# Requesting the third expert's weights together with the first two, before the routing ends

## The chip, the cores and the metric

The kernel runs on one core of a Trainium2 chip. The metric is the device time of one execution in microseconds, lower is better. The engines are TensorE (PE in the rows, its weight loads PEld), VectorE (DVE), ScalarE (ACT), GpSimd (POOL) and SyncE (SP). SyncE does nothing but wait and issue transfers here. Transfers of all queues run on the core's 16 DMA engines.

## The reference

Two layers over 256 context tokens and 512 latent tokens of width 1024. Each layer has a mixer (retention and a linear recurrence in the first, latent attention in the second) and then a hierarchical mixture of experts, in f32. Only the experts matter here:

```python
def hier_moe(h, group_w, group_b, expert_w, expert_b, w_gate, w_up, w_down):
    """h (T,D). Top-1 expert group, then top-2 experts inside it; exact sorted dispatch."""
    ...
    xin = h[row_tok].reshape(n_blocks, MOE_BLOCK, d)

    def expert_block(args):
        xb, e = args
        return (jax.nn.silu(xb @ w_gate[e]) * (xb @ w_up[e])) @ w_down[e]
```

There are 32 experts with a hidden width of 512, so each has three matrices of 2048 KB: gate, up and down. The first layer routes 768 tokens, the second the 512 latent tokens; each token goes to two experts. A block holds at most 128 rows.

## The kernel before

An expert layer is `moe_rows`. It reserves three buffers for each kind of weights (`expert_weights(s, 3)`: `moew_wg`, `moew_wu`, `moew_wd` in the rows) and calls `routing`, then `experts`.

**Routing.** VectorE works out which expert gets which token, with a few small matmuls in between, and last casts the list of tokens to integers (`all_tok`). SyncE has nothing to do but `prefetch`, which is the function `first` of `moe_rows`: it requests gate, up and down weights of experts 0 and 1, six transfers. At the end of the routing all engines meet.

**Experts.** The 32 experts are taken in order, one turn each, expert n in buffer n modulo 3 (q). Engines meet by semaphores only:

- GpSimd copies the indices of a turn (`exp_idx`) and issues an indirect transfer, the gather, that brings the expert's rows of `h_rows` to one of three buffers `xg` (in the space `all_hT`). It gathers 64 rows if the expert has 64 tokens or fewer, otherwise 128. `x_ready[q]` tells that they have landed. The first three gathers are issued at once, each further one when TensorE has transposed a buffer's rows.
- TensorE transposes the rows (`exp_xps`, line 1793), multiplies them with the gate and up weights (`exp_gps` and `exp_ups`, lines 1806 and 1807), transposes the rows of the next expert, then transposes the hidden rows (`exp_hps`) and multiplies them with the down weights (`exp_yps`, lines 1822 and 1824). Experts with 64 rows or fewer put the two products side by side on the array and take about half the time.
- ScalarE and VectorE form the hidden rows and copy results out of PSUM; ScalarE issues the store to `ys`.
- SyncE requests weights, through `load_gate_up` (line 1684, two transfers) and `load_down` (line 1690). Once TensorE is done with expert n's gate and up weights (`gu_used`), it requests those of expert n + 3 into the same buffer, and after `d_used` the down weights.

The weights of expert 2, the third, are requested at the head of SyncE's part of `experts`, behind a wait for the first gather:

```python
            sp.wait_ge(x_ready[0], 16)
            load_gate_up(sp, a, layer, w, S - 1, S - 1)
            load_down(sp, a, layer, w, S - 1, S - 1)
```

After the experts come `further_blocks` (for rows beyond 128 of an expert; the profile has no transfer of it) and `combine`, which gathers each token's two rows of `ys`.

Of the kernel before, what the change touches and what calls it, by code (L numbers as in the profile page):

```python
# [1668 lines left out]
def expert_weights(s, slots):  # L1669

    w = Box()
    w.g = [s.sb(f"wg{i}", [P, KD, HID]) for i in range(slots)]
    w.u = [s.sb(f"wu{i}", [P, KD, HID]) for i in range(slots)]
    w.d = [s.sb(f"wd{i}", [P, HT_N, DM]) for i in range(slots)]
    w.gu_ready = [s.sem(f"gu_ready{i}") for i in range(slots)]
    w.d_ready = [s.sem(f"d_ready{i}") for i in range(slots)]
    return w


def load_gate_up(sp, a, layer, w, e, q):  # L1680

    for buf, name in ((w.g, "moe_w_gate"), (w.u, "moe_w_up")):
        src = a[name][layer].rearrange("e (p k) n -> e p (k n)", p=P)[bass.ds(e, 1)]
        sp.dma_start(buf[q][:].rearrange("p k n -> p (k n)"), src.rearrange("o p m -> (o p) m")).then_inc(w.gu_ready[q], 16)


def load_down(sp, a, layer, w, e, q):

    src = a["moe_w_down"][layer].rearrange("e (p k) n -> e p (k n)", p=P)[bass.ds(e, 1)]
    sp.dma_start(w.d[q][:].rearrange("p k n -> p (k n)"), src.rearrange("o p m -> (o p) m")).then_inc(w.d_ready[q], 16)  # L1690


def experts(nc, c, a, layer, t0, r, w):
# [3 lines left out]
    with Scope(nc, f"exp{layer}") as s:  # L1697
        S = len(w.g)
# [18 lines left out]
        x_ready = [s.sem(f"x_ready{i}") for i in range(S)]  # L1717
# [24 lines left out]
        @block.sync  # L1742
        def _(sp):


            sp.wait_ge(x_ready[0], 16)
            load_gate_up(sp, a, layer, w, S - 1, S - 1)
            load_down(sp, a, layer, w, S - 1, S - 1)

            def turn(n, q, i):  # L1750
                sp.wait_ge(gu_used, n + 1)
                load_gate_up(sp, a, layer, w, n + S, q)
                sp.wait_ge(d_used, n + 1)
                load_down(sp, a, layer, w, n + S, q)

            with sp.Fori(0, E // S - 1) as i:
                for q in range(S):
                    turn(i * S + q, q, i)
            for n in range((E // S - 1) * S, E - S):
                turn(n, n % S, n // S)  # L1760
# [403 lines left out]
def moe_rows(nc, c, a, layer, t0, r):  # L2164

    with Scope(nc, f"moew{layer}") as s:
        w = expert_weights(s, 3)

        def first(sp):

            for e in range(len(w.g) - 1):
                load_gate_up(sp, a, layer, w, e, e)
                load_down(sp, a, layer, w, e, e)

        routing(nc, c, a, layer, t0, r, first)
        experts(nc, c, a, layer, t0, r, w)
    further_blocks(nc, c, a, layer, t0, r)
# [116 lines left out]
```

## Time and profile before

| | |
|---|---|
| median of 3 runs | 2321.19 us |
| lowest and highest | 2316.5 and 2325.09 us |
| profiled execution | 2321.44 us |
| its span, first to last instruction | 2319.8 us |
| mean granted TensorE clock | 0.919 of full speed |
| TensorE matmuls busy | 1889.0 us, 81% |
| VectorE busy | 716.2 us, 31% |
| weights requested by SyncE, 64 experts | three transfers of 2048 KB each |
| mean over the span | 246 GB/s of HBM traffic |

The profile is that of the profiled execution, and all times in rows are microseconds from its first instruction. The two expert layers take about half of the span. A queue's time from issue to landing includes the time that the transfer stood behind others.

### The profile page before, as it was taken

The numbers are of one execution on the slowest core, as the hardware profiler recorded it, in microseconds if no ns is written. First come the engines' busy times: TensorE is split into PE (matmuls) and PEld (weight loads), VectorE is DVE, ScalarE is ACT, GpSimd is POOL, SyncE is SP. The second block draws the span as 40 slices with busy tenths as digits, with TensorE's granted clock in tenths as the row PEclk, the third lists the DMA queues.
The fourth block names the chain that finished last, engine by engine and source line by source line (L and its number), as shares of the span: only waits on it lengthen the run. The fifth ranks groups of instructions, "written<-read, shape, count | busy, mean of one in ns | idle before, by whom it ended". The sixth has DMA issues, their size and how long they took to land. (4 is left out here: it accounts for less than half of the span.)

```text
span 2319.8 us, 23218 instructions
## 1 busy us (share of the span) xinstructions
PE 1889.0 (81%) x7918; PEld 982.4 (42%) x7919; DVE 716.2 (31%) x1243; ACT 429.8 (19%) x748; POOL 279.3 (12%) x355
## 2 busy tenths in 40 slices
PE   2559999889489999999853899999957989987781
PEld 0125444555334444444412546888533334433330
DVE  1130678553411111111227226555331111111114
ACT  2000233311001111111113114444201111111112
POOL 1020254211110000000014010000011000000001
PEclk9779999989689999999985899999968999998896
DMA  9971119210588999999963102000159999999993
GB/s 369 422 261 43 36 60 248 100 58 28 235 339 342 398 409 412 420 386 371 400 260 142 55 0 82 1 1 1 49 219 357 408 411 402 394 402 395 401 414 132
DMA packets 93246, 572.21 MB, mean 247 GB/s; under 512 B 21016, under 2 KB 35096, under 8 KB 61304
## 3 DMA queue, kind: packets, MB, share of 16 engines
q1 hardware_dynamic: 76864, 515.04, 56.7%
q0 software_dynamic: 8832, 30.68, 3.9%
q10 hardware_dynamic: 7480, 25.57, 2.8%
q8 instruction: 43, 0.70, 0.1%
q14 instruction: 27, 0.22, 0.0%
HBM read 529.47 MB, written 41.78 MB: 246 GB/s over the span
## 5 line engine op out<-in xcount | busy, mean ns | idle before, releaser
L1806 PE MATMUL exp_gps<-moew_wg,all_hT 128*64 128x512 f32 (+1 forms) x1024 | 486.1, 615 | 36.8 <-DMA moew_wu<-in_moe_w_up 34.7
L1807 PE MATMUL exp_ups<-moew_wu,all_hT 128*64 128x512 f32 (+1 forms) x1024 | 484.4, 613 | 0.0
L1806 PEld LDWEIGHTS exp_gps<-moew_wg,all_hT 128*64 128x64 f32 (+1 forms) x1024 | 153.4, 153 | 325.9 <-issue 321.0
L1822 PE MATMUL exp_yps<-moew_wd,all_hT 128*64 128x512 f32 (+1 forms) x512 | 243.7, 607 | 39.5 <-issue 39.5
L1824 PE MATMUL exp_yps<-moew_wd,all_hT 128*64 128x512 f32 (+1 forms) x512 | 244.2, 608 | 0.0
L1916 DVE TENSOR_TENSOR all_hT<-all_hT,exp_ups 64x512 f32<-64x512 f32 (+1 forms) x64 | 44.2, 691 | 586.4 <-ACT all_hT L1867 586.4
L1807 PEld LDWEIGHTS exp_ups<-moew_wu,all_hT 128*64 128x64 f32 (+1 forms) x1024 | 154.2, 153 | 50.9 <-issue 50.9
L577 PE MATMUL abp_ps<-abp_w,all_hT 128*128 128x512 f32 x384 | 166.8, 593 | 0.9 <-PE abp_ps L577 0.6
L1925 DVE COPY exp_y<-exp_yps 64x512 f32<-64x512 f32 (+1 forms) x64 | 44.3, 692 | 298.4 <-PE exp_yps L1824 298.4
L1822 PEld LDWEIGHTS exp_yps<-moew_wd,all_hT 128*64 128x64 f32 (+1 forms) x512 | 71.5, 149 | 147.9 <-issue 147.9
L1867 ACT ACTIVATE all_hT<-exp_gps 64x512 f32<-64x512 f32 (+1 forms) x64 | 37.8, 591 | 485.4 <-PE exp_ups L1807 485.4
L215 PE MATMUL ada_ps<-ada_w,ada_sT 128*32 128x512 f32 x384 | 63.2, 818 | 74.8 <-DMA ada_w<-in_ada_w 74.8
L577 PEld LDWEIGHTS abp_ps<-abp_w,all_hT 128*128 128x128 f32 x384 | 72.7, 190 | 93.7 <-issue 93.5
L1772 POOL COPY exp_idx<-all_tok 128x1 int32 (+1 forms) x64 | 11.7, 183 | 799.5 <-DVEq L1906 798.7
L1872 ACT COPY exp_y<-exp_yps 64x512 f32<-64x512 f32 (+1 forms) x64 | 37.2, 581 | 381.4 <-PE exp_yps L1824 381.4
L1321 PE MATMUL att_sc<-mla_KT,mlak_QT 96*128 96x384 f32 x256 | 98.0, 507 | 2.0 <-PEq L75 2.0
L581 PE MATMUL abp_ps<-all_hT,abp_w 128*128 128x256 f32 (+1 forms) x256 | 85.6, 498 | 15.8 <-DMA abp_w<-in_ab_w_in 15.5
L1793 PE MATMUL exp_xps<-all_ident,all_hT 128*128 128x128 f32 x512 | 74.5, 290 | 25.6 <-DMA all_hT<-h_rows,exp_idx 25.6
L1793 PEld LDWEIGHTS exp_xps<-all_ident,all_hT 128*128 128x128 f32 x512 | 64.3, 194 | 71.9 <-issue 46.0
L1332 PE MATMUL att_pv<-mla_V,mla_ckT 128*128 128x64 f32 x768 | 92.7, 271 | 0.0
L1332 PEld LDWEIGHTS att_pv<-mla_V,mla_ckT 128*128 128x128 f32 x768 | 90.7, 192 | 0.0
L1824 PEld LDWEIGHTS exp_yps<-moew_wd,all_hT 128*64 128x64 f32 (+1 forms) x512 | 72.5, 149 | 24.9 <-issue 24.9
(368 smaller groups left out, 2264.3 us busy)
## 6 DMA issues: line engine op xcount, KB each, us to landing
moew_wg<-in_moe_w_gate SPq DMA_DIRECT2D x64, 2048.0 KB, 23.1
moew_wu<-in_moe_w_up SPq DMA_DIRECT2D x64, 2048.0 KB, 29.0
moew_wd<-in_moe_w_down SPq DMA_DIRECT2D x64, 2048.0 KB, 27.7
ada_w<-in_ada_w SPq DMA_DIRECT2D x12, 4096.0 KB, 25.6
ys<-exp_y ACTq DMA_DIRECT2D x51, 256.0 KB, 8.3
abp_w<-in_ab_w_in SPq DMA_DIRECT2D x6, 2048.0 KB, 8.2
ys<-abp_zero SPq DMA_DIRECT2D x32, 256.0 KB
ys<-exp_y ACTq DMA_DIRECT2D x13, 512.0 KB, 10.1
```

The lines of the kernel that those rows point to most:

```text
L215: last = nc.tensor.matmul(ps[n % 2][32 * j:32 * j + 32, :], sT[:, k_, :], w[m % WB][:, kk, j * 512:(j + 1) * 512], start=(k_ == 0), stop=( ...
L577: last = nc.tensor.matmul(ps[i % RB][:], hT[:, kk, what * P:(what + 1) * P], w[n % S][:, kk, :], start=(kk == 0), stop=(kk == KD - 1))
L581: last = nc.tensor.matmul(ps[i % RB][:, 0:m], w[n % S][:, kk, ct * P:(ct + 1) * P], hT[:, kk, o:o + m], start=(kk == 0), stop=(kk == KD - 1))
L1321: last = nc.tensor.matmul(sc[n % 2][:, b, 0:HALF], k.QT[0:QD, h, t * P:(t + 1) * P], k.KT[0:QD, h, b * HALF:(b + 1) * HALF], start=True, s ...
L1332: last = nc.tensor.matmul(pv[n % 2][:, 0:VD], pT[n % 2][:, kt, :], k.V[:, kt, h * VD:(h + 1) * VD], start=(kt == 0), stop=(kt == NT - 1))
L1793: last = nc.tensor.transpose(xps[k // 4][:, k % 4, :], x_by[q][:, k, :], c.ident[:])
L1806: nc.tensor.matmul(gps[0:rows, :], x[:, k, 0:rows], w.g[q][:, k, :], start=(k == 0), stop=(k == KD - 1))
L1807: last = nc.tensor.matmul(ups[at:at + rows, :], x[:, k, 0:rows], w.u[q][:, k, :], start=(k == 0), stop=(k == KD - 1))
L1822: nc.tensor.matmul(yps[0][0:rows, :], hT[:, k, 0:rows], w.d[q][:, k, 0:512], start=(k == 0), stop=(k == HT_N - 1))
L1824: last = nc.tensor.matmul(yps[1][at:at + rows, :], hT[:, k, 0:rows], w.d[q][:, k, 512:1024], start=(k == 0), stop=(k == HT_N - 1))
L1916: nc.vector.tensor_tensor(h[at:at + rows, :], sg[at:at + rows, :], ups[at:at + rows, :], ALU.mult).then_inc(h_done, 1)
L1925: nc.vector.tensor_copy(y[q][0:rows, 512:1024], yps[1][at:at + rows, :]).then_inc(y_dve, 1)
```

## The change

The function `first` loops over all three buffers, so that nine transfers are requested during the routing, and the wait for the first gather and the requests behind it go from `experts`.

```diff
@@ -1742,11 +1742,6 @@
         @block.sync
         def _(sp):
 
-
-            sp.wait_ge(x_ready[0], 16)
-            load_gate_up(sp, a, layer, w, S - 1, S - 1)
-            load_down(sp, a, layer, w, S - 1, S - 1)
-
             def turn(n, q, i):
                 sp.wait_ge(gu_used, n + 1)
                 load_gate_up(sp, a, layer, w, n + S, q)
@@ -2168,7 +2163,7 @@
 
         def first(sp):
 
-            for e in range(len(w.g) - 1):
+            for e in range(len(w.g)):
                 load_gate_up(sp, a, layer, w, e, e)
                 load_down(sp, a, layer, w, e, e)
 
```

## Rows read from the trace of the kernel before

**Rows 1.** The page: TensorE's busy tenths and GB/s in 40 slices.

```profile
PE   2559999889489999999853899999957989987781
...
GB/s 369 422 261 43 36 60 248 100 58 28 235 339 342 398 409 412 420 386 371 400 260 142 55 0 82 1 1 1 49 219 357 408 411 402 394 402 395 401 414 132
```

**Rows 2.** TensorE's waits, 640 to 1195 us: total us, times, longest.

```profile
PE exp_xps L1793 <- DMA all_hT<-h_rows,exp_idx: 11.1, 1, 11.1
...
PE exp_gps L1806 <- DMA moew_wu<-in_moe_w_up: 0.9, 1, 0.9
```

**Rows 3.** SyncE's waits, 600 to 1300 us, same columns.

```profile
SPq L1684 <- PE exp_ups L1807: 261.1, 29, 18.1
```

**Rows 4.** Single stretches of the first layer; last columns clock, DMA share, GB/s.

```profile
637.00:641.00 4.00, 0.00 (x0) 0.00 (x0) 0.00 (x0) 0.00 (x0) 1.98 (x5) 0.50 0.00 0
720.00:730.00 10.00, 8.37 (x28) 4.36 (x27) 1.98 (x3) 1.19 (x2) 1.36 (x3) 1.00 0.46 165
1050.00:1060.00 10.00, 9.44 (x28) 4.47 (x26) 0.71 (x2) 1.13 (x2) 0.18 (x1) 1.00 0.86 342
```

**Rows 5.** TensorE's waits, 1840 to 2273 us.

```profile
PE exp_gps L1806 <- DMA moew_wu<-in_moe_w_up: 33.7, 11, 5.1
```

**Rows 6.** Two longer stretches, columns as in rows 4.

```profile
634.00:645.00 11.00, 0.72 (x4) 0.72 (x5) 0.00 (x0) 0.00 (x0) 6.01 (x12) 0.50 0.39 140
...
1748.00:2257.00 509.00, 434.82 (x1865) 186.68 (x1863) 78.72 (x125) 67.87 (x104) 37.52 (x87) 0.95 1.01 401
```

**Rows 7.** SyncE's requests in the first layer, start and duration; then one landing.

```profile
644.25 0.33 SPq L1684 DMA_DIRECT2D moew_wg<-in_moe_w_gate  x1
...
645.11 0.57 SPq L1690 DMA_DIRECT2D moew_wd<-in_moe_w_down  x1
664.18 0.35 SPq L1684 DMA_DIRECT2D moew_wg<-in_moe_w_gate  x1
...
681.57 0.33 SPq L1684 DMA_DIRECT2D moew_wg<-in_moe_w_gate  x1
...
moew_wd<-in_moe_w_down SPq DMA_DIRECT2D x1, 2048.0 KB, 20.7
```

**Rows 8.** Timeline of VectorE, POOL, TensorE; last, the fifteenth expert's first matmuls.

```profile
633.33 0.20 DVE L1666 CAST all_tok<-route_lps 128x43 int32<-128x43 f32 x1 [3.50 <-PE route_lps L1584]
...
639.60 1.19 POOL L1777 DMA_INDIRECT all_hT<-h_rows,exp_idx  x1 [1.56 <-issue]
...
644.28 1.98 PE L1793 MATMUL exp_xps<-all_ident,all_hT 128*128 128x128 f32 x8 [11.06 <-DMA all_hT<-h_rows,exp_idx]
...
647.34 1.22 PE L1806 MATMUL exp_gps<-moew_wg,all_hT 128*128 128x512 f32 x1 [1.08 <-DVE all_hT L1907]
...
893.25 1.02 PE L1806 MATMUL exp_gps<-moew_wg,all_hT 128*128 128x512 f32 x2
```

**Rows 9.** Landings of gathers issued at 639.6, 648.1, 838.4, 1738.3; all from 830 to 2100.

```profile
all_hT<-h_rows,exp_idx POOLq DMA_INDIRECT x1, 4.6
...
all_hT<-h_rows,exp_idx POOLq DMA_INDIRECT x1, 15.9
...
all_hT<-h_rows,exp_idx POOLq DMA_INDIRECT x1, 11.3
...
all_hT<-h_rows,exp_idx POOLq DMA_INDIRECT x1, 8.3
...
DMA to landing us min/median/max: 4.5/9.6/11.3
```

**Rows 10.** DMA packets from 1720 to 1738 us, and SyncE's queue alone.

```profile
DMA packets 535, 7.75 MB, mean 431 GB/s; under 512 B 62, under 2 KB 62, under 8 KB 62
...
q1 hardware_dynamic: 535, 7.75, 100.6%
```

**Rows 11.** The stretch of the second layer's first gathers, columns as in rows 4.

```profile
1743.00:1750.00 7.00, 2.28 (x10) 1.87 (x12) 0.69 (x1) 0.93 (x2) 1.28 (x3) 0.50 0.73 185
```

**Rows 12.** SyncE's requests in the second layer, and the landing of the first shown.

```profile
1747.46 0.42 SPq L1690 DMA_DIRECT2D moew_wd<-in_moe_w_down  x1
1759.73 0.35 SPq L1684 DMA_DIRECT2D moew_wg<-in_moe_w_gate  x1
...
moew_wd<-in_moe_w_down SPq DMA_DIRECT2D x1, 2048.0 KB, 19.3
```

## The prediction

> **What bounds the kernel now.** The change touches the two expert layers only, so I read the page for their place first: the GB/s line has two long stretches near 400 GB/s [rows 1]. They are the first expert layer, from 605 us on, and the second, from 1711 us on. The share of busy time cannot say which of two engines sets the end, so each layer is read by its waits.
>
> First layer: TensorE waited for DMA once at length, 11.1 us before its first transposes, and that was the gather of the first expert's rows; for weights it waited once in 555 us, 0.9 us [rows 2]. SyncE, in turn, sat 261.1 us waiting for TensorE to release gate/up buffers [rows 3], and the DMA share is 0.46 and 0.86 in single slices, the later one at 1050 to 1060 us [rows 4]: all three buffers were full and the queue was empty. So the first layer is paced by TensorE. A start of TensorE that is d later makes the layer end d later, and weights that lie ready earlier are worth nothing.
>
> Second layer: TensorE waited 33.7 us in 11 waits for the up weights after 1840 us [rows 5], and the DMA share from 1748 to 2257 us is 1.01 at 401 GB/s [rows 6]. It is paced by the transfers. Transfer time saved at its start is worth its full length, and a TensorE start a little later is worth nothing as long as the next request still finds the queue filled.
>
> **The change, part by part.** It removes one wait (SyncE, for the first gather) and moves three requests of 2048 KB per layer to before the routing's end. Nothing computed changes, no buffer is added.
>
> *The issues themselves.* Three issues of 0.33 to 0.57 us on SyncE [rows 7], 1.3 us, move to right behind the sixth, at 608.4 us, and SyncE is through by about 610. Routing goes on until VectorE's cast of the token list at 633.3 us [rows 8], and SyncE only waits for its end: cost 0. Without that cover it would be 1.3 us a layer. They pass no other request on SyncE's queue; what they get ahead of are POOL's gathers.
>
> *The first gather of the first layer.* Before, it found an empty queue: the share is 0.00 from 637 to 641 us [rows 4], and the gather issued at 639.60 landed after 4.6 us [rows 9]; TensorE's transposes began at 644.28 [rows 8]. After, 18.87 MB (nine times 2048 KB) are asked for by 610 us; at the 431 GB/s of a pure weight stream [rows 10] that is 43.8 us, so weights run until about 650 us and the gather shares the 16 engines with them from the start. Gathers issued under a filled queue took 9.6 us in the median of a long stretch, 11.3 at most; the 11.3 belongs to the fifteenth expert, which like the first has the 128-row form [rows 8, 9]. I take 11.3, the nearest row: **+6.7 us**. Bounds: below, 8.3 us, the second layer's first gather, which met weights only for its first half: +3.7. Above, 15.9 us, a gather with others just ahead of it: +11.3 [rows 9]. A gain is excluded, since 4.6 us is the gather on an empty queue. The term is on the path, since the whole first layer follows TensorE.
>
> The Trainium skill (DMA: Bandwidth & Descriptors, section Queues, rings and completion order) says that each DMA engine takes turns between the queues that have work for it, and lets one whole packet of some 9 to 17 descriptors through before it switches. That speaks against the change, which puts weights on the same engines as the gather. If one request's share on an engine is one such packet, an estimate by that page is 4.3 us of delay (8 pieces of 16 KB at 0.54 us) and a sum of 2322.9. The measured gathers took longer than that, and the sum goes by them.
>
> *The third expert's weights, first layer.* The last of them lands at about 650 us, in place of 645.11 + 20.7 = 665.8 [rows 7]. TensorE releases the second expert's gate/up buffer only at 681.57 [rows 7] and can't use the third's before, so they were early already: 0. DMA stood idle for (1 - 0.39) x 11 = 6.7 us between 634 and 645 us [rows 6]; that idle time goes here and comes back where the buffers are full. If that cover were gone (a layer paced by weights) it would be -6.7.
>
> *The third expert's weights, second layer.* The gather is what they waited for until 1746.6 us. From 1743 to 1750 us the share is 0.73 at 185 GB/s [rows 11]. By share, 7 x 0.27 = 1.9 us were idle; by bytes at the mixed rate that follows [rows 6], 7 x (1 - 185/401) = 3.8 us. A gather's packets are slower per byte, so the truth lies between; I take the middle, **-2.8 us**, bounds -1.9 and -3.8. It is on the path, as the layer stays paced by transfers to its end.
>
> *The first gather of the second layer* now meets weights for its whole life: 9.6 in place of 8.3 us, +1.3 on TensorE's first turn [rows 9]. Hidden, if the queue doesn't run dry: the third down weights landed at 1747.46 + 19.3 = 1766.8 [rows 12], now 2.8 us earlier, 1764.0. The fourth expert's request came at 1759.73 [rows 12], now 1761.0, still 3.0 us before that. If this cover were gone, the gain would shrink by what is missing.
>
> **Sum.** +6.7 - 2.8 = +3.9 us. The profiled execution took 2321.44 us (a span of 2319.8 and 1.6 around it), the median of the three runs is 2321.19, so the two agree. 2321.4 + 3.9 = **2325.3 us**, slower by 0.17%.
>
> **Rivals.**
> *A, nearly a wash.* The gather waits for one request's share of weights and no more. 535 weight packets carried 7.75 MB in 18 us of 16 engines [rows 10], so a request of 2.1 MB has 9 on an engine, 0.54 us each: +4.9 us, and with the saving by bytes 4.9 - 3.8 = +1.1, 2322.5 us. It is also where the page's rule above leads. For it: the second layer's first gather, 8.3 us. Against: the 11.3 and the 9.6 us.
> *B, the gather gets stuck.* 15.9 us as the gather issued at 648 us: +11.3 - 2.8 = +8.5, 2329.9 us. For it: a queue filled to 650 us. Against: it has no gather ahead of it, as that one had, and the steady ones come through a queue just as deep.
> *C, faster.* The first layer is paced by weights after all, so that the 6.7 us of idle DMA are gained and the late gather is hidden: -6.7 - 2.8 = -9.5, 2311.9 us. It decides from the point at which TensorE's lead over the weights (15 us at the third expert: 681.57 less 665.8) is used up before the queue first runs empty. Against: the slice of share 0.46 at 720 to 730 us [rows 4].
> *D, it does only the half that costs.* In the second layer the queue runs dry at 1761 us and the saving is lost there: +6.7, 2328.1 us. For it: a margin of 3.0 us only.
>
> **How the numbers follow.** Forecast (+2.5 to +6.5, that is 2323.9 to 2327.9) 0.48; A 0.22; B 0.12; C 0.05; D 0.13. The runs before lie from 4.7 below their median to 3.9 above it, so a median scatters by 3 or 4 us beside the terms. Range: A less 4.5 gives 2318, B plus 1 gives 2331; outside it are C and the far ends of the scatter. A measurement of this kernel tells about 0.5%, 11.6 us, from no change (2309.6 to 2332.8): faster 0.03 (C with scatter), slower 0.04 (B with scatter), within 0.93.
>
> **What the profile would show.** Right: nine requests from 605 to 610 us; weights without a pause to about 650 us; the first gather issued at 639.6 and landing near 650.9; the first gate/up matmul near 654.0 (647.34 [rows 8]); the fourth expert's request near 670.9 (664.18 [rows 7]); all later requests of that layer late by the same 6.7 us. Second layer: a share near 1 from 1743 to 1750 us (plus the shift), its first gather at 9 to 10 us, and the layer 2 to 4 us shorter. Wrong would be: a first gather under 8 or over 14 us; a shift that shrinks along the first layer (weights did pace it); a gap in the share where the fourth expert's request of the second layer is made; or a TensorE clock that rises at another point of the first turn, which began at half speed and could move the whole layer by a microsecond or two.

## The result

The changed kernel took 2330.44 us in the median of 7 runs (2327.69 to 2332.39), the kernel before 2321.19 (2316.5 to 2325.09): a ratio of 1.0039 with a 95% interval of 1.0026 to 1.0051, slower by about 9 us and short of the 0.5% that was named as the bound. The forecast was 2325.3 us, in a range of 2318 to 2331.

The profiled execution has a span of 2328.5 us, 8.7 more than before. Its difference comes from few places: the first expert layer is 7.5 us longer than before and the second 0.4; the rest (0.6 us up to the first request, -0.5 between the layers, 0.8 at the end) is spread over stages that the change doesn't touch.

**The requests.** SyncE's queue after, in order of time, start and duration; before, the third expert's three stood at 644 us [rows 7].

```profile
605.66 0.34 SPq L1684 DMA_DIRECT2D moew_wg<-in_moe_w_gate  x1
...
608.48 0.45 SPq L1690 DMA_DIRECT2D moew_wd<-in_moe_w_down  x1
608.97 0.48 SPq L1684 DMA_DIRECT2D moew_wg<-in_moe_w_gate  x1
609.49 0.46 SPq L1684 DMA_DIRECT2D moew_wu<-in_moe_w_up  x1
609.99 0.48 SPq L1690 DMA_DIRECT2D moew_wd<-in_moe_w_down  x1
671.90 0.35 SPq L1684 DMA_DIRECT2D moew_wg<-in_moe_w_gate  x1
```

The nine are out by 610.5 us and nothing waits for SyncE: the routing's end is later by 0.6 us, as its start is. The fourth expert's request is the number to look at: 671.90, where before it was 664.18 [rows 7], 7.7 us later.

**The first gather.** Timeline of POOL and TensorE after, to hold against [rows 8].

```profile
640.18 1.19 POOL L1772 DMA_INDIRECT all_hT<-h_rows,exp_idx  x1 [1.56 <-issue]
...
652.18 1.97 PE L1788 MATMUL exp_xps<-all_ident,all_hT 128*128 128x128 f32 x8 [18.37 <-DMA all_hT<-h_rows,exp_idx]
655.23 2.07 PE L1801 MATMUL exp_gps<-moew_wg,all_hT 128*128 128x512 f32 x2 [1.08 <-DVE all_hT L1902]
```

The landing of this gather after, as in [rows 9]:

```profile
all_hT<-h_rows,exp_idx POOLq DMA_INDIRECT x1, 11.9
```

TensorE's waits from 640 to 1203 us after, as in [rows 2]:

```profile
PE exp_xps L1788 <- DMA all_hT<-h_rows,exp_idx: 18.4, 1, 18.4
PE exp_gps L1801 <- DVE all_hT L1902: 1.1, 1, 1.1
```

The gather took 11.9 us to land in place of 4.6, and TensorE waited 18.4 us for it in place of 11.1: 7.3 us, and no wait for weights came in its place anywhere in the layer. Where the time goes inside the gather is seen when the packets are counted by queue, first from its issue to 644 us, then from 644 to 652 us (packets, MB, share of the 16 engines; q0 is the gathers' queue, q1 SyncE's):

```profile
DMA packets 115, 1.62 MB, mean 427 GB/s; under 512 B 16, under 2 KB 16, under 8 KB 16
...
q1 hardware_dynamic: 115, 1.62, 100.3%
...
q1 hardware_dynamic: 175, 2.61, 79.9%
q0 software_dynamic: 166, 0.61, 19.4%
```

In the 3.8 us behind the issue not one gather packet ran, only weights; then gather packets alternated with weights, at a fifth of the engines' time. Before, on the empty queue, the first six gather packets lay in the 2.0 us behind the issue:

```profile
DMA packets 6, 0.02 MB, mean 12 GB/s; under 512 B 0, under 2 KB 0, under 8 KB 6
...
q0 software_dynamic: 6, 0.02, 8.4%
```

In narrower windows the first gather packet is found 4.5 us behind the issue, where it was 1.9 before. So 2.6 of the 7.3 us pass before the gather's first packet, and the other 4.7 while its packets take turns with weights. Why the first packet is late by 2.6 us no run shows.

**The stretches.** Columns as in [rows 4, 6]: engines' busy time, granted clock, DMA share, GB/s.

```profile
637.00:641.00 4.00, 0.00 (x0) 0.00 (x0) 0.00 (x0) 0.00 (x0) 2.01 (x4) 0.50 0.98 418
728.00:738.00 10.00, 8.37 (x29) 4.43 (x28) 1.98 (x3) 1.19 (x2) 1.36 (x3) 1.00 0.45 159
...
656.00:668.00 12.00, 12.00 (x24) 5.11 (x23) 0.00 (x0) 0.67 (x1) 0.98 (x1) 0.82 0.15 49
1757.00:2265.00 508.00, 430.48 (x1864) 186.25 (x1862) 78.75 (x125) 67.85 (x104) 37.65 (x87) 0.96 1.01 400
```

The hole of 637 to 641 us is filled (0.98), and another has opened at 656 to 668 (0.15), with all three buffers full; the later hole is as deep as before (0.45 at 728 us for 0.46 at 720). The second layer runs at 1.01 and 400 GB/s, as before.

### The profile page after: what moved, and what is told of

Read it like the earlier page. It is cut to its first block and busy times, and to the rows that moved or that the text cites. A ratio compares the mean times of both kernels' runs of the same rounds, so it can differ in the third digit from the quotient of the medians.

```text
span 2328.5 us, 23218 instructions
## 1 busy us (share of the span) xinstructions
PE 1887.7 (81%) x7918; PEld 982.6 (42%) x7919; DVE 716.7 (31%) x1243; ACT 429.7 (18%) x748; POOL 279.6 (12%) x355
## 5 line engine op out<-in xcount | busy, mean ns | idle before, releaser
L1801 PE MATMUL exp_gps<-moew_wg,all_hT 128*64 128x512 f32 (+1 forms) x1024 | 481.0, 609 | 39.5 <-DMA moew_wu<-in_moe_w_up 37.1
L1802 PE MATMUL exp_ups<-moew_wu,all_hT 128*64 128x512 f32 (+1 forms) x1024 | 479.4, 608 | 0.0
L215 PE MATMUL ada_ps<-ada_w,ada_sT 128*32 128x512 f32 x384 | 65.8, 848 | 72.6 <-DMA ada_w<-in_ada_w 72.6
L1788 PE MATMUL exp_xps<-all_ident,all_hT 128*128 128x128 f32 x512 | 74.5, 290 | 34.5 <-DMA all_hT<-h_rows,exp_idx 34.5
```

What stands on the lines that cost most here:

```text
L215: last = nc.tensor.matmul(ps[n % 2][32 * j:32 * j + 32, :], sT[:, k_, :], w[m % WB][:, kk, j * 512:(j + 1) * 512], start=(k_ == 0), stop=( ...
L1788: last = nc.tensor.transpose(xps[k // 4][:, k % 4, :], x_by[q][:, k, :], c.ident[:])
L1801: nc.tensor.matmul(gps[0:rows, :], x[:, k, 0:rows], w.g[q][:, k, :], start=(k == 0), stop=(k == KD - 1))
L1802: last = nc.tensor.matmul(ups[at:at + rows, :], x[:, k, 0:rows], w.u[q][:, k, :], start=(k == 0), stop=(k == KD - 1))
```

## The experiments

All kernels are edits of the kernel before. From each profile I read the same four numbers of each layer: how long the first gather took to land, and, counted from the layer's first weight request, when TensorE began its first transposes, when the fourth expert's weights were requested, and when the last down matmul ended. The time of the gather's issue, 34.4 to 34.5 us in the first layer unless an experiment moves it, is named where it matters. For the kernels before and after, these ends are in the timeline of TensorE, the last two starts of each plus 0.59 us:

```profile
1192.98 0.59 PE L1824 MATMUL exp_yps<-moew_wd,all_hT 128*64 128x512 f32 x1
...
2271.81 0.59 PE L1824 MATMUL exp_yps<-moew_wd,all_hT 128*64 128x512 f32 x1
```

```profile
1201.05 0.59 PE L1819 MATMUL exp_yps<-moew_wd,all_hT 128*64 128x512 f32 x1
...
2279.74 0.59 PE L1819 MATMUL exp_yps<-moew_wd,all_hT 128*64 128x512 f32 x1
```

| kernel | ratio to before (95%) | first layer: gather, transposes, fourth's request, end | second layer: the same |
|---|---|---|---|
| before | | 4.6, 39.2, 59.1, 588.5 | 8.3, 35.6, 48.7, 561.3 |
| the change | 1.0039 (1.0026 to 1.0051) | 11.9, 46.5, 66.2, 596.0 | 9.9, 37.2, 49.4, 561.7 |
| e1, first layer only | 1.0025 (1.0014 to 1.0036) | 11.9, 46.5, 65.9, 594.5 | 7.7, 34.9, 47.4, 561.7 |
| e2, second layer only | 1.0002 (0.9992 to 1.0012) | 4.6, 39.1, 59.1, 585.7 | 11.0, 38.3, 50.0, 563.8 |
| e3, gate and up early | 1.0028 (1.0016 to 1.0039) | 10.7, 45.3, 65.6, 592.1 | 11.0, 38.2, 50.0, 561.2 |
| e4, only the wait gone | 1.0034 (1.0022 to 1.0046) | 11.0, 45.5, 65.8, 595.0 | 10.7, 38.0, 51.1, 560.6 |
| e5, first layer's gather held | 1.0030 (1.0018 to 1.0041) | 4.7, 47.2, 66.6, 596.2 | 7.5, 34.7, 47.5, 559.8 |
| e6, e2 and its gather held | 1.0032 (1.0017 to 1.0047) | 4.6, 39.1, 59.1, 588.0 | 9.7, 45.0, 57.5, 566.0 |
| e7, gate early | 1.0012 (1.0002 to 1.0022) | 5.4, 39.8, 59.5, 589.1 | 10.9, 38.2, 50.8, 562.8 |
| e8, clears shared | 0.9996 (0.9984 to 1.0008) | 4.6, 38.6, 57.5, 585.6 | 8.7, 35.4, 47.2, 561.4 |
| e9, third late, first layer | 1.0005 (0.9991 to 1.0019) | 4.6, 39.1, 60.9, 586.3 | 8.5, 35.7, 48.7, 563.5 |
| e10, third late, second layer | 1.0054 (1.0037 to 1.0071) | 4.6, 39.2, 58.8, 588.5 | 7.8, 35.0, 49.0, 573.2 |
| e11, first clear only | 0.9999 (0.9986 to 1.0012) | 4.6, 37.4, 56.8, 586.1 | 10.5, 36.0, 49.1, 562.3 |

A layer that is left as it was varies from profile to profile. The first took 585.7 to 588.5 us in e2, e6, e10 and before; the second 559.8 to 561.7 in e1, e5 and before, and 563.5 in e9. Differences below 3 or 4 us in one layer say nothing by themselves.

**e1 and e2: one layer each.** In which of the two layers is the loss made?

```diff
-            sp.wait_ge(x_ready[0], 16)
-            load_gate_up(sp, a, layer, w, S - 1, S - 1)
-            load_down(sp, a, layer, w, S - 1, S - 1)
+            if layer != 0:          # e2: if layer != 1
+                sp.wait_ge(x_ready[0], 16)
+                load_gate_up(sp, a, layer, w, S - 1, S - 1)
+                load_down(sp, a, layer, w, S - 1, S - 1)
...
-            for e in range(len(w.g) - 1):
+            for e in range(len(w.g) - (layer != 0)):          # e2: layer != 1
```

> The change is made in the first expert layer alone; the second requests the third expert's weights behind the first gather, as before. Theory (the first gather of the first layer shares the engines with weights, lands after 11.9 us in place of 4.6, and TensorE, which paces that layer, carries it to the end): the first layer ends 7 to 8 us later, the second takes what it took before, 2329 us, ratio 1.0032 to 1.0037. Rival (part of the 9 us is made in the second layer): 2325 us, ratio about 1.0018, and the first layer's end under 5 us later.

> The change is made in the second expert layer alone. Theory (there the idle share before the third request is small, 1.2 us at the landing of the third down weights, and is lost again later): the layer is 0 to 1.2 us shorter, 2320.5 us, ratio 0.9995 to 1.0000. Rival 1 (the forecast's saving is there in full): 2.8 us shorter, 2318.4 us, ratio 0.9988. Rival 2 (its own late gather costs something): 1 to 2 us longer, ratio 1.0005 to 1.0008. First gather 9 to 10 us to landing in all three.

e1 carries the loss: transposes at 46.5 us, as with the whole change, and a first layer of 594.5 us. That is 6.0 us longer than before, where 7 to 8 were expected and under 5 by the rival. Its ratio of 1.0025 is below what was expected (1.0032 to 1.0037), but its interval reaches into that and holds the rival's 1.0018 too; the profile, with the transposes late by 7.3 us and the second layer at 561.7, decides for the first layer. e2 is at 1.0002 in time, and its layer took 563.8 us, with a gather that landed after 11.0 us. The forecast's saving of 2.8 us (ratio 0.9988) isn't there: the interval of e2 starts above it, at 0.9992. For the layer 0 to 1.2 us less was expected and the profile shows 2.5 more, inside what such a layer varies. A small cost of its own late gather (the second rival, 1.0005 to 1.0008) isn't excluded by the time; the profiles with the full change in that layer (560.6, 561.7 and 563.8 us in e4, the change and e2) don't show one beside those without it (559.8 to 563.5).

**e3, e7 and e4: how much is queued, and since when.** e3 requests gate and up of the third expert during the routing, e7 the gate alone; the rest stays behind the wait. e4 leaves all three at the head of the experts' part and takes only the wait away.

```diff
 e3, first(); e7 requests only the gate here, and the up behind the wait:
             for e in range(len(w.g) - 1):
                 load_gate_up(sp, a, layer, w, e, e)
                 load_down(sp, a, layer, w, e, e)
+            load_gate_up(sp, a, layer, w, len(w.g) - 1, len(w.g) - 1)
 e3, experts():
             sp.wait_ge(x_ready[0], 16)
-            load_gate_up(sp, a, layer, w, S - 1, S - 1)
             load_down(sp, a, layer, w, S - 1, S - 1)
 e4, experts():
-            sp.wait_ge(x_ready[0], 16)
             load_gate_up(sp, a, layer, w, S - 1, S - 1)
             load_down(sp, a, layer, w, S - 1, S - 1)
```

> In both layers only the third expert's gate and up are requested during the routing, its down weights wait for the first gather as before: 16.78 MB ahead of the gather in place of 18.87. In the first layer weights then run to about 645 us. Theory (the delay is the time during which gather packets alternate with weight packets): the gather meets weights for 3 to 4 us of its life and lands after 7.5 to 9 us, the layer ends 3 to 4.5 us later, 2324.5 us, ratio 1.0012 to 1.0020. Rival (what counts is a filled queue at the moment of issue): 11 to 12 us to landing and the whole 7 to 8 us, ratio 1.0032.

> Only the third expert's gate is requested during the routing, its up and down behind the first gather. In the first layer weights then run out at about 641 us, a microsecond behind the gather's issue. Theory (weights that are still queued while the gather runs make the delay): first packet of the gather barely later, 5 to 7 us to landing, the layer ends 0.5 to 2 us later, ratio 1.0002 to 1.0010. Rival (any filled queue at the moment of issue costs the full delay): 10 to 12 us to landing, ratio 1.0028.

> Only the wait is taken away: the third expert's weights are requested at the head of the experts' part, at about 634 us, behind the routing and 5 us ahead of the gather's issue. Theory (the weights on the engines during the gather make the delay, whenever they were requested): gather lands after 11 to 12 us, as with the change, 2328 to 2330 us, ratio 1.0030 to 1.0040. Rival (the requests during the routing themselves cost, by nine filled requests on the queue or by slowing the routing): near the kernel before, ratio under 1.0015.

e4 is the change without the early requests: they go out at 634.84 to 635.69 us, 5 us ahead of the gather, and it lands after 11.0 us, the ratio 1.0034. So it isn't the time of the request that costs, nor anything that nine requests do during the routing, but weights on the engines while the gather is on its way.

e7, with 14.7 MB ahead, lands its gather after 5.4 us, as its theory said, and its layer is 0.6 us longer; the ratio, 1.0012, is just above the expected 1.0002 to 1.0010, which its interval holds. e3, with 16.8 MB, doesn't fit its theory: 10.7 us, where 7.5 to 9 were expected for a gather that meets weights for half its life and 11 to 12 for the rival. Its ratio is 1.0028 for an expected 1.0012 to 1.0020. The packets by queue from e3's gather issue to 646 us, and from e7's to 641.9 us, tell why:

```profile
DMA packets 124, 1.77 MB, mean 432 GB/s; under 512 B 16, under 2 KB 16, under 8 KB 16
...
q1 hardware_dynamic: 124, 1.77, 101.4%
```

```profile
q1 hardware_dynamic: 49, 0.66, 78.5%
q0 software_dynamic: 6, 0.02, 9.2%
```

In e3 no gather packet ran for 4.1 us, in e7 they began within 2.0 us. The first packet of e3's gather came 4.3 us behind the issue, 2.4 us later than on an empty queue, and with the change 2.6 us later; taking turns with weights comes on top. So that first part is nearly the same in e3, whose last weight packet ran 7.5 us behind the gather's issue, and with the change, where it ran 14.8 us behind. In e7, where it ran 2.6 us behind, there is no such delay. The theory of e3, a delay by the time of overlap alone, was wrong: holding back only the down weights saved 1.2 us of landing.

**e5 and e6: only a late gather.** Eight more clears on POOL hold the first gather back, 8.0 us, without any transfer.

```diff
             pool.wait_ge(xg_set, S)
 
+            if layer == 0:          # e6: if layer == 1, on top of e2
+                for m in range(8):
+                    nc.gpsimd.memset(xg[0], 0.0).then_inc(xg_set, 1)
+                    pool.wait_ge(xg_set, S + m + 1)
+
```

> The kernel before with eight more clears of the first gather's buffer ahead of it on POOL, in the first layer only: some 7.3 to 8 us that hold back the gather and touch no weight request (the third's stays behind the gather's landing). Theory (a late first gather is all it takes in the layer that TensorE paces): the first layer ends later by what the gather lands later, the second is unchanged, 2330.5 us, ratio 1.0032 to 1.0036, as with the change. Rival (the first layer has slack, and the change costs by contention of its transfers): ratio under 1.0015.

> The change in the second layer alone, with the same eight clears there. Theory (weights pace that layer, so a late first turn is hidden as far as the queue is filled): the fourth expert's request comes some 57.5 us after the first, the third's down weights land at 55.6, so 2 to 3.5 us of the 7.3 to 8 are lost and the layer takes 565 to 567 us from its first request, ratio 1.0010 to 1.0015. Rival (the second layer follows TensorE's start as the first does): 569 to 572 us, ratio 1.0032.

The timeline of e5, POOL then TensorE:

```profile
638.05 8.02 POOL L1772 MEMSET all_hT<- 128x1024 f32 x8
...
648.41 1.19 POOL L1782 DMA_INDIRECT all_hT<-h_rows,exp_idx  x1 [1.55 <-issue]
...
653.13 1.97 PE L1798 MATMUL exp_xps<-all_ident,all_hT 128*128 128x128 f32 x8 [19.16 <-DMA all_hT<-h_rows,exp_idx]
```

The gather lands in 4.7 us, on a free queue, but late; transposes begin at 47.2 us (39.2 before), the layer ends at 596.2, and the ratio is 1.0030 (1.0032 to 1.0036 was expected, 1.0015 at most by the rival). A late gather alone does to this layer what the change does. The third expert's weights, which wait for the gather, are late too, but e9 below shows that this costs nothing. From first transposes to the end, the first layer takes 549.3 us before, 549.5 with the change, 549.0 in e5 and 548.9 in e6, and 546.6 to 549.5 in all thirteen: within these 3 us, which are scatter, the start passes through in full.

In e6 the second layer's transposes begin 6.8 us later than in e2, and the layer is 2.2 us longer than e2's (4.7 longer than before). It takes 566.0 us, where the theory had 565 to 567 and the rival 569 to 572. The queue runs dry where it was expected to, between the third's last landing at 53.9 us (55.6 was expected) and the fourth's request at 57.5 us. In e6's stretch around that request the DMA share is 0.29:

```profile
1766.00:1772.00 6.00, 5.24 (x30) 2.38 (x26) 1.38 (x2) 1.17 (x2) 0.36 (x2) 1.00 0.29 62
```

The layer's length fits the theory. The timed ratio, 1.0032 (1.0017 to 1.0047), excludes the 1.0010 to 1.0015 expected and equals the rival's; its profiled execution is 6.9 us over the one before, of which this layer accounts for 4.7 and the stages before the first expert layer for 2.3. So profile and time don't agree, and how much of a late gather the second layer hides stays open; that it hid some of it rests on one profile.

**e9 and e10: weights late in place of early.** The third expert's weights are requested only when TensorE has released the first expert's gate/up.

```diff
             sp.wait_ge(x_ready[0], 16)
+            if layer == 0:          # e10: if layer == 1
+                sp.wait_ge(gu_used, 1)
             load_gate_up(sp, a, layer, w, S - 1, S - 1)
```

> The kernel before, with the third expert's weights of the first layer requested only when TensorE has released the first expert's gate/up, about 20 us later than before (664 in place of 644 us). Theory (TensorE paces this layer, the third's weights have over 20 us of lead): the layer takes 585 to 589 us from its first request as in the unchanged ones, ratio 0.999 to 1.001. Rival (their arrival does matter): up to 20 us longer, ratio above 1.003.

> The same in the second layer: third expert's weights requested at about 48.5 us after the first request in place of 35.5, 13 us later. Theory (transfers pace this layer to its end): the engines stand idle for these 13 us and the layer takes 571 to 575 us in place of 561, ratio 1.0045 to 1.006. Rival (the missing saving of the change means that the layer is not paced by transfers): within 3 us of 561, ratio under 1.0015.

This is the cleanest pair. 20 us later, the weights cost nothing in the first layer (586.3 us, 1.0005); 12 us later, they cost 11.9 us in the second (573.2 for 561.3, 1.0054). The stretch in which e10 has nothing to transfer but gathers:

```profile
1742.00:1757.00 15.00, 12.83 (x52) 5.80 (x52) 2.08 (x3) 3.05 (x4) 1.66 (x5) 0.75 0.21 55
```

So the first layer is paced by TensorE and the second by transfers, and idle time of the DMA engines is lost in full there.

**e8 and e11: an earlier gather.** If a late first gather costs its full length, an earlier one should pay. Before it, POOL clears all three buffers, 2.7 us. e8 moves two clears to VectorE but lets the gather wait for all; e11 lets it wait for its own.

```diff
 e11 (e8 keeps the one wait for all three):
-            for x in xg:
-                nc.gpsimd.memset(x, 0.0).then_inc(xg_set, 1)
-            pool.wait_ge(xg_set, S)
+            nc.gpsimd.memset(xg[0], 0.0).then_inc(xg_first, 1)
+            pool.wait_ge(xg_first, 1)
...
+                if q:
+                    pool.wait_ge(xg_set, S - 1)
...
+            for x in xg[1:]:
+                nc.vector.memset(x, 0.0).then_inc(xg_set, 1)
```

> The kernel before with two of the three clears ahead of the first gather moved from POOL to VectorE, in both layers, so that the gather is issued 1.8 us earlier. Theory (the first layer follows the first gather's landing in both directions): that layer ends 1.8 us earlier, the second is within 0.5 us of before, 2321 us, ratio 0.9992. Rival (another engine or the weights hold the first turn by then): no change of the first layer's length.

> The kernel before, both layers: the first gather waits for the clear of its own buffer alone, the other two buffers are cleared by VectorE and waited for only by their own gathers. The gather is issued 1.8 us earlier in each layer. Theory (first layer follows the first gather's landing): transposes begin about 37.4 us after the first request in place of 39.2, and the layer takes 1.8 us less; the second layer as before; 2320 us, ratio 0.9990 to 0.9994, which the timing can hardly tell from 1. Rival (with the gather earlier it meets the last of the second expert's weights, which run to 32 us, and lands later by as much): transposes at 39 us, ratio 1.0000.

e8's gather was to be issued 1.8 us earlier, and was not: VectorE makes its two clears one after the other, 0.91 us each from 636.17 us on, and POOL waited for the second until 638.50, so the gather was issued only 0.5 us earlier (34.0 for 34.5). In e11 it is earlier by 1.8 us: 32.7 us, transposes at 37.4 in place of 39.2, the first layer 586.1 us. In the second layer the earlier gather meets more weights (10.5 us to landing), and the transposes begin no earlier than before. The time, 0.9999 (0.9986 to 1.0012), can't tell 1.8 us from nothing; no kernel here is measurably faster than the one before.

## Why the prediction was right, and what in it was not

- *What paces each layer.* Right, both. e5 and e9 show it for the first (a late gather costs in full, late weights nothing), e10 for the second. Rival C, a first layer paced by weights, is out. TensorE's clock, which the prediction named as a danger, stayed out of it: in the first layer the granted clock left 0.50 some 8 us behind the first transposes both before and after (in the slices from 652 and from 660 us), in the first expert's gate and up products.
- *The issues at cost 0.* Right: e4, which has them at another place, behaves as the change.
- *The first gather of the first layer, +6.7 us.* The mechanism and place were right, the size was 7.3. Rival B's landing after 15.9 us did not come, nor rival A's delay of only 4.9 us. By the rule of the Trainium skill that was set beside it (DMA: Bandwidth & Descriptors, Queues, rings and completion order) the prediction's estimate was 4.3 us of delay. It took 0.54 us a piece, a mean that counts 62 tiny packets as well; the 473 pieces of 16 KB took 18 x 16 / 473 = 0.61 us each [rows 10], so eight give 4.9 us. The trace agrees with the taking of turns but has 7.3 us, 2.6 of which pass before the first gather packet.
- *The third's weights early, first layer, 0.* Right: the hole in the DMA share moved to 656 us. The weights ran to 655 us, though, not to 650: the 43.8 us had left out the first microsecond and the engine time of the three gathers.
- *The third's weights early, second layer, -2.8 us.* This is the step that failed, the term "7 x 0.27" and "7 x (1 - 185/401)". The layer took 561.7 us, not 558.5. The forecast looked at 7 us only. The same 7 us after, 32 to 39 us behind the first request:

```profile
1750.50:1757.50 7.00, 1.69 (x8) 1.57 (x8) 0.00 (x0) 0.00 (x0) 0.92 (x1) 0.50 1.00 317
```

  The rate there rose from 185 to 317 GB/s, 0.92 MB more, worth 2.3 us at 401 GB/s. But part of the gathers' work had only moved to later: they brought 0.57 MB in these 7 us before and 0.42 after. The 20 us from 30 to 50 us behind the first request hold nearly the same gather bytes (1.05 MB before, 1.04 after) and show what was left, before and then after:

```profile
1741.00:1761.00 20.00, 12.88 (x48) 5.42 (x48) 1.41 (x3) 2.82 (x4) 3.62 (x8) 0.64 0.91 306
```

```profile
1748.60:1768.60 20.00, 11.71 (x47) 5.07 (x48) 0.70 (x2) 2.46 (x3) 3.45 (x7) 0.65 1.01 328
```

  The share rose from 0.91 to 1.01, that is 2.0 us of engine time, but the rate only from 306 to 328 GB/s: 0.44 MB more, worth 1.1 us at 401 GB/s. While gathers and weights are in flight together the engines are busy and slow: weights had 84.4% of the engines for 5.51 MB in these 20 us, that is 0.80 us a piece of 16 KB, before 0.72, and 0.61 alone. Both estimates had valued the hole as if it would be filled at the normal rate. The third's down weights landed 54.5 us behind the first request, 1.2 us earlier than before (55.7). Over more profiles it is about the same: 54.5 to 55.6 with the full change there (the change, e2, e4), 55.7 to 56.9 in the six without any early request in that layer (before, e1, e5, e8, e9, e11), means of 55.1 and 56.3. Whether it lasts to the end of the layer stays open: the layer's length varies by more, and the three profiles with the full change there have 560.6, 561.7 and 563.8 us.
- *The first gather of the second layer, hidden.* Right: 9.9 us to landing (9.6 forecast); the fourth's request came at 49.4 us, 5.1 us ahead of the third's last landing, so the queue did not run dry. Rival D gave a total of 2328.1 us, nearer to the measured than the forecast, but by another mechanism, which did not occur. e6, with the gather issued 8 us later, shows the queue running dry.
- *The sum.* +3.9 was forecast. With the terms as measured in the profile it is +7.5 and +0.4; the timed difference of 9 us has an interval from 6 to 12 us, so +3.9 lies outside it. The likeliest case's own range, to 2327.9, missed. The whole range, to 2331, held, and that was in part luck: its upper end came from rival B, whose total of 2329.9 us is the nearest of all to the measured 2330.44, but whose delay of 11.3 us did not occur.

## What to carry to other kernels

- A wait that seems to delay a prefetch for nothing may keep the path free for a small transfer that everything else waits for. Before removing it, look for the transfer that the consumer waits for first, and ask what will be on the DMA engines during its life; here 12.6 MB ahead of it cost nothing and 18.9 MB cost 7 us.
- Two layers of the same code can have different bounds. Read the bound of each (who waits for whom, and whether the DMA share ever falls). A late first gather counts in full only where TensorE sets the pace, and idle time of the DMA engines only where the transfers do.
- An idle share of the DMA engines isn't time that a prefetch gains: check at which rate the hole would be filled, beside the gathers that are in it, and whether their work only moves to later.

## What the runs showed of the hardware

- A first gather of 128 rows landed in 4.6 us on an empty queue (4.7 in e5), in 10.7 to 11.9 us under a stream of weights (the change, e1, e3, e4), and in 5.4 us where the last weights ran 2.6 us behind its issue (e7). Under the stream its first packet ran 4.3 to 4.6 us behind the issue; before, in e5 and in e7, 1.9 to 2.0 us.
- In the second layer a first gather of 64 rows under such a stream took 9.7 to 11.0 us (the change, e2, e3, e4, e6, e7), hardly less than one of 128 rows in the first. No run changes the size alone.
- A full DMA share carried 427 GB/s with weights alone, 403 GB/s with gathers among them in the first layer (644 to 652 us after), and 328 GB/s in the 20 us around the second layer's first gathers. What sets it within that range no run shows.
